# Head-norm squares on ScalarE, negated attention scores, and 71 matmul jobs whose activation operand has 512 columns

## The reference, cut to what matters

```
h = rms_norm(x) ; z = h @ w_in -> glu_in, q, k, v, gate_logits
a = a_val * sigmoid(a_gate) ; a = causal_depthwise_conv(a, width 31)
y_a = silu(rms_norm(a)) @ w_conv_out
q = rms_norm(q per head of 64) / 8 ; k = rms_norm(k per head of 64)
o = three dilated windows of attention with ALiBi, mixed by their log-sums
x = x + (g_a * y_a + g_b * (o @ w_attn_out)) @ w_out
h = rms_norm(x) ; u = depthwise_conv(h @ w_up, width 3)
x = x + (silu(u_gate) * u_val) @ w_down
```

```
h = h + mix @ w_out ; u = rmsnorm(h)
h = h + (silu(u @ ffn_w_gate) * (u @ ffn_w_up)) @ ffn_w_down
return rmsnorm(h, final_norm)
```

## Time and profile before

| | us |
|---|---|
| median of three runs | 899.05 |
| the profiled execution | 898.74 |
| its span, first to last instruction | 896.9 |
| PE busy | 854.5 (95%) |
| DVE busy | 635.5 (71%) |
| ACT busy | 551.7 (62%) |
| POOL busy | 320.4 (36%) |

### The profile page before, as it was taken

How to read it: one execution, slowest core, us unless ns; L and a number is a source line. 1 busy time by engine, 2 the same in 40 slices (tenths; PEclk the granted TensorE clock), 3 DMA queues, 4 the chain that set the end, 5 groups by cost and what they waited for, 6 DMA issues and landing times.

```text
span 896.9 us, 18034 instructions
## 1 busy us (share of the span) xinstructions
PE 854.5 (95%) x6762; PEld 832.9 (93%) x6762; DVE 635.5 (71%) x1071; ACT 551.7 (62%) x993; POOL 320.4 (36%) x308
## 2 busy tenths in 40 slices
PE   4999888999999999999999999999999999999996
PEld 3998888999999899999999988999999999999996
DVE  5988899798587789778665758747577844444542
ACT  5677876788665676666545676466646655555441
POOL 3799996334523234333111210001033233333111
PEclk9999998999999999999999999999999999999998
DMA  5564454344456546565565535435345565554741
GB/s 202 200 201 181 145 168 142 113 141 130 159 166 188 160 124 218 183 187 185 177 209 188 160 112 172 123 114 172 114 144 180 155 207 184 185 189 143 219 132 48
DMA packets 42310, 146.21 MB, mean 163 GB/s; under 512 B 4704, under 2 KB 7024, under 8 KB 42224
## 3 DMA queue, kind: packets, MB, share of 16 engines
q1 hardware_dynamic: 41472, 143.67, 50.3%
q10 hardware_dynamic: 752, 1.39, 0.4%
HBM read 144.00 MB, written 1.05 MB: 162 GB/s over the span
## 4 chain that ended last, share of the span: by engine, by line
PE 76%; DVE 12%; issue 4%; ACT 4%; POOL 3%; DMA 1%; DVEq 0%; ACTq 0%; POOLq 0%
PE px L508 23%; PE px L509 22%; PE px L510 22%; DVE wlo L1316 3%; DVE px L1375 2%; PE px L550 1%; ACT whi L846 1%; PE px L572 1%; PE px L707 1%; POOL CA L1890 1%; DVE sq L1331 1%; POOL wlo L1841 1%; DVE hx L1337 1%; PE px L514 1%; PE px L516 1%
## 5 line engine op out<-in xcount | busy, mean ns | idle before, releaser
L508 PE MATMUL px<-hx,whi 128*128 128x256 f32 x1392 | 403.2, 290 | 10.2 <-DVE hx L1337 6.1
L509 PE MATMUL px<-hx,whi 128*128 128x256 f32 x1392 | 395.1, 284 | 0.0
L510 PE MATMUL px<-hx,wlo 128*128 128x256 f32 x1392 | 395.0, 284 | 0.0
L1316 DVE TENSOR_TENSOR wlo<-raw,whi 128x1024 fp32r<-128x1024 f32 x251 | 324.9, 1301 | 66.4 <-ACT whi L846 66.0
L846 ACT ACTIVATE whi<-raw 128x1024 fp32r<-128x1024 f32 x267 | 279.8, 1051 | 66.0 <-PE px L510 49.3
L508 PEld LDWEIGHTS px<-hx,whi 128*128 128x128 f32 x1392 | 268.3, 193 | 15.6 <-DVE hx L1337 7.6
L509 PEld LDWEIGHTS px<-hx,whi 128*128 128x128 f32 x1392 | 268.5, 193 | 0.4
L510 PEld LDWEIGHTS px<-hx,wlo 128*128 128x128 f32 x1392 | 268.2, 193 | 0.0
L1890 POOL TENSOR_TENSOR CA<-CA,ct 128x256 f32<-128x256 f32 x90 | 85.9, 955 | 50.2 <-ACT ct L913 42.4
L1964 POOL TENSOR_TENSOR fx<-tt,fx 128x256 fp32r<-128x256 f32 x40 | 56.4, 1413 | 129.3 <-ACT fx L1107 129.3
L509 PE MATMUL px<-fx,whi 128*128 128x256 f32 x352 | 99.6, 283 | 0.0
(11 more groups left out here) (285 smaller groups left out, 1301.5 us busy)
## 6 DMA issues: line engine op xcount, KB each, us to landing
raw<-ws SPq DMA_DIRECT2D x267, 512.0 KB, 3.7
tb<-tabs SPq DMA_DIRECT2D x16, 128.0 KB, 2.4
out<-X SPq DMA_DIRECT2D x4, 256.0 KB, 2.4
X<-xs SPq DMA_DIRECT2D x1, 512.0 KB, 4.9
X<-xs ACTq DMA_DIRECT2D x1, 512.0 KB, 5.1
vc<-vecs ACTq DMA_DIRECT2D x1, 320.0 KB, 7.0
msk<-lmask ACTq DMA_DIRECT2D x1, 256.0 KB, 2.8
ug<-pos ACTq DMA_DIRECT2D x1, 128.0 KB, 4.3
```

What stands on the lines that cost most here:

```text
L508: e.matmul(b[:, 0:S], H, xh, start=first, stop=False)
L509: e.matmul(b[:, 0:S], H, xl, start=False, stop=False)
L510: m = e.matmul(b[:, 0:S], L, xh, start=False, stop=end)
L1316: e.tensor_tensor(wlo[:, n % NSL, :], raw[:, n % NRAW, :], whi[:, n % NSL, :], ALU.subtract).then_inc(s_lov, 1)
```

## The change

Five edits. They are independent of each other, except that the two about squares and scores fall in the same stretch.

1. For 71 jobs (`dn`, `wo`, `wo2` all eight each, `fd` all but the last, `fg` and `fu` from the third on) PE multiplies the high weights with high and low activations in one instruction of 512 columns, and the low weights with the high ones in one of 256 columns. Main product and corrections lie in the two halves of the bank. One DVE instruction more adds the second half: in a residual job a second addition to `X`, behind a wait for the first; in `fg` and `fu` an addition to the copied tile, which now frees the bank in place of ACT's copy.
2. The squares for the head norms are made by ACT from the bank, ahead of its copy, and no longer by POOL from the copy.
3. Scores are made negative by negative scale factors in `q` (and in the second block's rotary tables) and negated distance tables; DVE takes a minimum, which is the negated maximum; the instruction that negated it and its semaphore are gone, and ACT's exponential has a scale of -1.
4. `SILUS` has the eight blocks in three jobs (3, 3, 2) instead of four (2, 2, 2, 2), and the last two low halves are made in the last `ao` job and not behind it.
5. Constants follow: negative factors in `qg8` and the rotary tables.

```diff
+WIDE = ({("dn", i) for i in range(KD)} | {("fd", i) for i in range(KD - 1)} | {("wo", i) for i in range(KD)} |
+        {("wo2", i) for i in range(KD)} | {(k, i) for k in ("fg", "fu") for i in range(2, FT)})
...
-            return [(t[:, i, 0, :], t[:, i, 1, :]) for i in range(n)]
+            return [(t[:, i, 0, :], t[:, i, 1, :], t[:, i, :, :].rearrange("p a s -> p (a s)")) for i in range(n)]
...
-        SILUS = {3: (0, 1), 4: (2, 3), 5: (4, 5), 6: (6, 7)}
+        SILUS = {3: (0, 1, 2), 4: (3, 4, 5), 5: (6, 7)}
...
-                    xh, xl = xs[k]
+                    xh, xl, both = xs[k]
                     first, end = k == 0, k == kt - 1
-                    if w == 1:
+                    if key in WIDE:
+                        b = banks[0]
+                        e.matmul(b[:, :], H, both, start=first, stop=False, skip_group_check=True)
+                        m = e.matmul(b[:, S:2 * S], L, xh, start=False, stop=end, skip_group_check=True)
+                    elif w == 1:
...
@@ scalar, qkg(m) @@
                     e.wait_ge(s_mm, ENDS[w, i])
+                    if m >= 3:
+                        e.wait_ge(s_hsum, m - 2)
+                    e.activation(hsq[:, m % 3, :], px_of[(w, i), 0][:, 0:S], ACT.Square).then_inc(s_hsq, 1)
...
@@ scalar, exps @@
-                e.wait_ge(s_max[a], h + 1)
+                e.wait_ge(*BANK["sc", a, h])
...
-                e.activation(sP_[:, j, 0:S], sS_[:, j, 0:S], ACT.Exp, bias=mx_[:, h, 2:3], accum_out=mx_[:, h, 4:5])
+                e.activation(sP_[:, j, 0:S], sS_[:, j, 0:S], ACT.Exp, scale=-1.0, bias=mx_[:, h, 2:3],
+                             accum_out=mx_[:, h, 4:5])
...
@@ scalar, second feed-forward @@
-                        e.activation(buf, px_of[keys[n], 0][:, 0:S], ACT.Copy).then_inc(BANK[keys[n], 0][0], 1)
+                        e.activation(buf, px_of[keys[n], 0][:, 0:S], ACT.Copy).then_inc(s_t1, 1)
...
@@ vector, softmax @@
-                e.tensor_tensor_reduce(sS_[:, j, 0:S], b[:, 0:S], T, 1.0, -3e38, ALU.add, ALU.max, mx_[:, h, 0:1])
-                e.tensor_tensor_reduce(sS_[:, j, S:384], b[:, S:384], T[:, P:S], 1.0, -3e38, ALU.add, ALU.max,
-                                       mx_[:, h, 1:2]).then_inc(BANK["sc", a, h][0], 1)
-                e.wait_ge(*BANK["sc", a, h])
-                e.tensor_scalar(mx_[:, h, 2:4], mx_[:, h, 0:2], -1.0, None, ALU.mult).then_inc(s_max[a], 1)
+                e.tensor_tensor_reduce(sS_[:, j, 0:S], b[:, 0:S], T, 1.0, 3e38, ALU.add, ALU.min, mx_[:, h, 2:3])
+                e.tensor_tensor_reduce(sS_[:, j, S:384], b[:, S:384], T[:, P:S], 1.0, 3e38, ALU.add, ALU.min,
+                                       mx_[:, h, 3:4]).then_inc(BANK["sc", a, h][0], 1)
...
@@ vector, residual @@
+                if key in WIDE:
+                    e.scalar_tensor_tensor(out=X[:, i, :], in0=px_of[key, 0][:, S:2 * S], scalar=0.5, in1=X[:, i, :],
+                                           op0=ALU.mult, op1=ALU.add).then_inc(s_cor, 1)
+                    corrected[0] += 1
+                    e.wait_ge(s_cor, corrected[0])
...
@@ vector, second feed-forward, row(n) @@
                     elif f:
+                        e.wait_ge(s_t1, 2 * FT + n - 3)
+                        e.tensor_tensor(buf, buf, b[:, S:2 * S], ALU.add).then_inc(done, 1)
                         return
...
@@ gpsimd, qkg(m) @@
-                if w in "qk":
-                    buf = QR[i % 4] if w == "q" else K[:, i, :]
-                    e.wait_ge(*BANK[(w, i), 0])
-                    if m >= 3:
-                        e.wait_ge(s_hsum, m - 2)
-                    e.tensor_tensor(hsq[:, m % 3, :], buf, buf, ALU.mult).then_inc(s_hsq, 1)
```

More of the change, by code:

```diff
@@ L396, in two_blocks @@
         s_hsq, s_hsum, s_hr, s_hsc = sem("s_hsq"), sem("s_hsum"), sem("s_hr"), sem("s_hsc")
-        s_sc, s_max, s_exp, s_rec, s_nrm, s_tr, s_pv, s_ohi = (
-            [sem(f"{n}{a}") for a in range(2)] for n in ("s_sc", "s_max", "s_exp", "s_rec", "s_nrm", "s_tr", "s_pv", "s_ohi"))
+        s_sc, s_exp, s_rec, s_nrm, s_tr, s_pv, s_ohi = (
+            [sem(f"{n}{a}") for a in range(2)] for n in ("s_sc", "s_exp", "s_rec", "s_nrm", "s_tr", "s_pv", "s_ohi"))
         s_ca, s_ctanh, s_cg, s_chi, s_clo = (sem(n) for n in ("s_ca", "s_ctanh", "s_cg", "s_chi", "s_clo"))
@@ L1472, in _ @@
                     taps(CONV_END + 1)
-            for n in SILUS[6]:
-                conv_low(n)
             def mix(a, key, i, GA_, GB_, other):
@@ L2063, in shape_constants @@
         slope = 2.0 ** (-8.0 * (h + 1) / NH)
-        tabs[h] = np.where(count > 0, lc - slope * d, NEG)
-    tabs[NH] = np.where(d >= 0, 0.0, NEG)
+        tabs[h] = -np.where(count > 0, lc - slope * d, NEG)
+    tabs[NH] = -np.where(d >= 0, 0.0, NEG)
     j, i = np.arange(P)[:, None], np.arange(P)[None, :]
```

14 lines of the change are left out of this document (8 added, 6 removed).

## The result

The changed kernel takes 890.11 us (median of four runs, 888.88 to 892.86); the kernel before took 899.03 us on the same chip (897.34 to 900.3). The ratio is 0.9906, 95% interval 0.9878 to 0.9934. It is faster by 8.9 us where 17.3 us were forecast, and lies outside both ranges, my own (877 to 885) and, by 0.1 us, the wide one (871 to 890). The profiled execution took 888.88 us, its span 886.9, and from here on spans and stages are compared.

The account below looks back on a forecast made before the run. PE's pace was taken as the bound for most of the program, DVE from 88 to 158 us. 898.7 - 10.4 (wide matmul) - 5 - 0.5 (stage, tail) - 1.4 (SiLU) = 881.4, median 881.7 us; own range 877 to 885, wide 871 to 890.

Parts of the forecast that it names:

- wide matmul: In `dn`, `fd`, `wo`, `wo2`, `fg`, `fu`: 778 blocks each lose 13.3 ns, 10.4 us in all.
- The stage, 5.5 us with its tail: `q`, `k` jobs and first heads, 88 to 158 us: DVE relieved, 5 us less; 0.5 us more up to 215 us.
- the unseen form: Rival: going from a 512 to a 256 keeps wide blocks near 0.36 us; 890 to 892 us, chance 0.07.
- The negation's part: Between 88 and 158 us: six two-element DVE instructions go, 3.2 us of DVE's time; later ones give 0.5 us.
- My 2 us for the squares: Between 88 and 158 us: with squares off POOL, DVE's instructions are stretched less, 2 us of DVE's time.
- Everything dissolves: Rival, `q`, `k` and first heads: stalls and clock fall vanish, stage gives 12 to 15 us; 871 to 875 us, chance 0.12.
- SiLU, 1.4 us: Start of `co`: last low halves come a job (2.9 us) earlier, so PE's wait goes, 1.4 us gained.
- the second addition: Residual jobs, `fg` and `fu`: the extra DVE instruction costs 0, at most 1.5 us at the ends of three stages.
- the slower rival: `fg` and `fu`: DVE frees banks late and each of 40 jobs pays, 24 us; 905 us, chance 0.05.
- ACT did not become the bound: Rival, `q` and `k` jobs: ScalarE (ACT) takes DVE's place, the stage gives 0; 887 us, chance 0.14.

Follow-up runs that it names:

- e1: Kernel before with only the wide matmuls (512-column operand in 71 jobs, second additions): 892.28 us, ratio 0.9927.
- e6: Kernel before with only the negated scores, DVE taking a minimum and the negation gone: 893.34 us, ratio 0.9954.
- e14: Changed kernel, POOL making only 8 of 1024 columns of its low chunks from the first `q` job on, results incomplete: 877.49 us, ratio 0.9755.
- e12: Changed kernel with the first head's minimum one job earlier, on DVE alone: 889.37 us, ratio 0.9892.
- e17: Changed kernel with DVE, not POOL, making the low parts of all chunks from the first `q` job on: 881.06 us, ratio 0.9809.
- e5: Changed kernel word for word, one more execution with its profile: 890.69 us.

## Why the prediction was wrong

The profiles differ by 10.0 us where the stages of the forecast sum to 17.3. The 7.3 us between them are: wide matmul 2.2, the stage of `q`, `k` and heads 1.9, `ao` and `co` 1.2, the fall of the clock in `wo2` 1.5, latent and linear attention 0.7, less the 0.2 that the start gained.

**The wide matmul, 10.4 us: right mechanism, too large.** Every removed matmul does give time back, and all of it is on the path; but the 13 ns a block that I took come only in `fg` and `fu`, and there only in three profiles of fifteen. The twelve others have 7 ns there, and `dn` and `fd` have 10 ns in all fifteen. The step that failed is "256 more columns cost 0.1067 us, exactly their time", taken from jobs whose neighbours are of 512 columns too. Between 256s the 512 takes 0.230 or 0.236 us, and the 256 gives 2 to 3 ns back. A block of `fg` is 0.345 to 0.347 or 0.353 us, one of `fd` and `dn` 0.350. At 7 ns a block the term is 778 x 7 ns = 5.4 us, at 13 it is 10.4. e1 measured 6.6 by its ratio and 6.2 by its stages; the changed kernel's own profile, one of the three, has 8.2. I had named the unseen form as a rival's reason and gave it 0.07, where it deserved a value between the ends. The Trainium skill ("TensorE: Matmul & The Clock Gate", "Back-to-back issue gap"), by which the gap beyond the columns' time is 2.5 ns, is no nearer: the 512 lies 17 to 23 ns beyond 213. The same section of the Trainium skill gives that figure for an isolated matmul, without the weight load that stands ahead of every matmul here.

**The stage, 5.5 us with its tail: 3.6.** The negation's part held by its ratio (4.1 us, e6). The step that failed is "A quarter of POOL's work goes (14.1 of 58.8), so I put 2 us to it", and before it the sum of busy times. DVE's loss to POOL is not a share of POOL's busy time. It is paid by each DVE instruction that reads SBUF alone and meets a POOL instruction, up to about that one's end, and the costly ones are POOL's `wlo` of 2.3 us and more. The squares accounted for 3.0 of DVE's 15.7 us of excess. With them gone the total is 14.1. Since 2.2 of the 15.7 had lain on the negation, the other instructions lose 14.1 us where they had lost 13.5: the scalings met the long ones more (17.6 to 20.3 us). My 2 us for the squares were 0 or less. e14 shows what the long instructions that stayed cost: 9.5 us of the stage (134.67 to 125.14). "Everything dissolves" was possible, but not by these edits.

The rule of the Trainium skill that I quoted ("SBUF — State Buffer", "Who interferes with whom": VectorE and GpSimd share a port pair, "and it's an exclusive lock") was the right rule, but I read it as an average. Read by instruction it says which POOL work to move. The traces agree with it: scalings take 0.47 to 0.49 us without POOL and 2.55 us under its `wlo`. POOL waits as well: its `wlo` at 114.13 us in the changed kernel, which begins under one of DVE's, takes 3.39 us where the shortest takes 2.35.

**The lead lost at a bank.** I named what the relief would bring, but not what is late next: the second head's scores, whose bank is held through two jobs. It could be seen before: one of the two waits of the earlier trace rows stood there, and I built only on the other. Since 3.7 us of lead turned into a stall of 7.35 us, the clock fell again (0.89 in the window, as before), and PE paid for that a second time. The bank was only where the lateness showed: e12 took it away, and PE stood for 6.1 us four heads on.

**SiLU, 1.4 us: 0 to 0.2.** The step that failed is "They come a job (2.9 us) earlier". Halves that could be made a job earlier still stand in line on DVE behind `wlo`, and DVE has hardly a gap in those jobs (busy for 14.3 of the 15.2 us from 234 us to PE's wait). I said "what is late next is the first `co` matmul's own chunk" without looking at what is ahead of the low halves on DVE. POOL's long chunks have a part in this too: with them cut short (e14) PE does not wait at `co`, and `ao` and `co` last 47.2 us and not 49.0; with them on DVE (e17) it is 48.1.

**Right:** the second addition costs nearly nothing (`wo` gave 0.4 us for 0.45 to 0.85 by its blocks; PE waits 0.4 us at that stage's start, as it did before). The 40 additions in `fg` and `fu` took 0.42 us each and no PE wait names them, so the slower rival did not come. ACT did not become the bound.

**Falls of the clock that vary.** Besides the one at the span's end, each profile has one to five stretches at the 1.2 GHz level, of some 3.4 or 6.8 us and once, in e5, of 10.2. A stretch of 3.4 us costs some 1.7 us. The one behind the stall of 6.8 to 7.4 us came each time, in six profiles; those near 31, 98, 250, 300 to 313, 540 to 552 and 658 to 675 us came in some profiles and not in others with the same stalls. Profiles of one kernel can thus differ by 2 to 3 us in their stages. The 1.5 us at 670 us is such a fall, and part of what is missing between the profile's sum and mine.

## What to carry to other kernels

Price contention between DVE and POOL by the instruction: look for DVE instructions that last much longer at some times than at others, and for the POOL instructions that they meet. Where a few of those are long, move these first, even onto the engine that is late. A gain in front of a shared bank or a fixed order is only a lead; follow it to the next instruction that waits, and count it when the stage's end moves. Take a matmul's pace from its own neighbours, and for a sequence that no row shows put the value between the bounds.
